# Two transformer blocks on one core: a token-major first norm, gates that read stored tiles in halves, and a delayed start of the head groups

## The chip, the cores and the metric

One Trainium2 chip; the program runs on one of its cores. The metric is the device time of one execution in microseconds (us), median of several. The engines are PE (TensorE, the matmuls), DVE (VectorE), ACT (ScalarE), POOL (GpSimd) and SP (SyncE); "ACTq" and "SPq" in the rows are the instruction streams of ACT and SP where they issue a DMA. Line numbers with an L are those of the kernel before, unless a sentence says otherwise.

## The reference, cut to what matters

The input x is 1024 tokens of 1024 features. The first block is a norm, a mixer of five branches A to E with a gate for each, and a residual; the second block has an even layer (dilated attention of four heads, pooling, a memory attention) and an odd layer. What the change touches:

```
h = rms_norm(x, g_pre)                      # x * rsqrt(mean(x*x) + 1e-6) * g_pre
...
y_d = _rglru(conv(d_x), ...) * silu(d_z)    # D: a recurrence over the tokens
mem_kv = rms_norm(mem, g_mem) @ w_mem_kv
es = einsum('bshd,bmhd->bhsm', eq, mk) * XATTN_HEAD_DIM ** -0.5
y_e = einsum('bhsm,bmhd->bshd', softmax(es), mv) * silu(e_z)
gate = sigmoid(gates)                       # 5 branches x 1024
merged = sum(gate * einsum('bsnw,nwd->bsnd', ys, w_br))
x = x + rms_norm(merged @ w_out, g_post)
...
for g in range(3):                          # even layer, each head: windows 128, 512, 2048
    num[g], m[g], den[g] = dilated_window_group(rope(q[g]), rope(k[g]), v, ...)
wts = exp(m - max(m)); out = sum(wts * num) / sum(wts * den)
y_a = out * silu(z)
```

Everything is float32.

## The kernel before

**Tiling.** Most tensors lie feature-major in SBUF: a tile is 128 features by 1024 tokens, and eight tiles (KD = 8) make x, h or the sum `acc`. `wt(j)` is tile j of the workspace `wrk` (eleven tiles), `wt(j, b)` is its half b of 512 tokens. PE works on two halves: a dense product of one weight tile (8 slices of 128 rows) is 8 steps for half 0 and 8 for half 1. Each value and each weight is split in two parts, hi and lo, and each step is three matmuls of 128x512 (hi by hi, lo by hi, hi by lo, L346), so a weight tile is 48 matmuls. The dense products write PSUM banks 0 and 1; transposes, attention and norms use banks 2 to 7. SP loads one 512 KB weight tile after the other into two slots (`w_raw`), and POOL splits them (L2327, L2332) as PE takes them.

**Order.** Nothing is reordered at run time. The program is a list of sections; a section has three threads, `dense`, `aux` and `side`, each a row of stages with a planned length in microseconds. Each engine's instruction stream is made by merging the threads by their planned times (`play`); a `yield` fraction inside a stage sets its due time. A planned length is therefore no duration; it says only what stands ahead of what. Each engine takes its stream in order, so that a matmul that waits holds all matmuls behind it, dense ones of another thread too.

**Start.** ACT issues the constants (`cst`), 37 small loads (rows of biases, gains and conv weights into `wt(0)`, `a_log`, `a_dt_bias`), then eight token-major tiles of x. After a drain (L898) PE turns the rows (L910) and then the x tiles, 8 transposes each (L917), and DVE copies them to `acc` (L927). ACT stores `acc` to DRAM as `x_fm`. Then a feature-major norm of each half: ACT squares (L504), PE sums over the features by a matmul with ones (L521), ACT takes the root (L507), DVE the reciprocal of a 128x512 tile (L529), then per feature tile DVE scales (L566), ACT rounds to the hi part (L579), DVE takes the lo part (L559). The first dense product ("A beta alpha", one weight tile) follows each part; then the two memories are turned (L1171, 8 transposes for 128 memory rows, loaded by L873), and "A project" begins (12 weight tiles).

**Gates of D and E.** Silu of z was computed before and stored to a DRAM scratch `away`. `gate_stored` (L1002) loads eight pieces of 128x512 back one by one (L1015) into the two halves of `wt(10)`; piece i waits for the multiply of piece i-2. DVE multiplies (L1025) and makes `y_hi` (L1027) and `y_lo` (L1028), and counts `y_done`; PE's y products wait for it. The D gate shares its section with E's attention: its inputs come by six fetches of 512 KB (L873), its scores are L782, its softmax L810. The E gate follows in the next section, where DVE also works out rotary angles.

**The post norm's x.** One load of `x_fm` brings x back to `wt(0..7)`, feature-major, ahead of the residual's add.

**Heads.** Four sections, one per head h: `dense` has the head's z product (one tile, Silu on ACT, L1984, into `y_spare`) and the next head's q, k and v (seven tiles); `side` has the rope on DVE (L1809 to L1813); `aux` has three attention groups and then `dilated_join` (L1888). A group turns v on PE (L1845), copies it (L1849), and runs eight attention steps (scores L782, Exp with row sum on ACT L810, transposes L795, value products L1873). The join spreads maxima over partitions (PE L1899, 24 matmuls), copies them (ACT), takes the joint maximum (DVE L1926 to L1929), the weights (ACT Exp), spreads the denominators (PE L1899, 24 more), and joins on DVE (L1941 to L1962). The next head's first L1845 waits for the join's end.

```
i = min((d, j) for j, d in enumerate(due) if d is not None)[1]   # L2287, in words: the thread with the lowest planned time goes next
```

## Time and profile before

| | us |
|---|---|
| median of 3 runs | 4007.83 |
| lowest, highest | 4007.68, 4010.31 |
| profiled execution, its own time | 4009.19 |
| span of that execution | 4007.4 |
| PE busy | 3528.8 (88%) |
| DVE / POOL / ACT busy | 1816.5 / 1577.4 / 919.5 |
| mean granted PE clock | 0.946 |

The profiled execution is 1.8 us longer than its span and 1.4 us above the median. "Idle before" in a row is the time in which the engine had nothing between its last instruction and this one; the name behind the arrow is what ended the wait. Busy time of a pipelined matmul overlaps the next, so a run of dense matmuls is read from the distance of their starts.

### The profile page before, as it was taken

Reading aid. Unit: us, or ns where it says so; the run is one execution under the profiler, and the core shown is the slowest. Engines: PE = TensorE matmul, PEld = TensorE weight load, DVE = VectorE, ACT = ScalarE, POOL = GpSimd, SP = SyncE. Lnnn points to the kernel's source line nnn. Section 1 sums busy time; section 2 is a strip of 40 time slices with the busy share of each in tenths; the row PEclk is TensorE's granted clock in tenths of the full one; section 3 lists DMA queues with packets and bytes.
Section 4 is the critical chain, followed back from the end, with each engine's and each line's share of the span. In section 5 each row is a group of like instructions: output and inputs, shape, how many; then the busy total and the mean of one; then the engine's idle time right before and its main releaser. Section 6 shows DMA issues by size and latency. Waiting matters only on the chain.

```text
span 4007.4 us, 44134 instructions
## 1 busy us (share of the span) xinstructions
PE 3528.8 (88%) x16700; PEld 2816.8 (70%) x16700; DVE 1816.5 (45%) x2349; ACT 919.5 (23%) x1687; POOL 1577.4 (39%) x2013
## 2 busy tenths in 40 slices
PE   5898999998998899979799699669677988989988
PEld 3677898886875667757577377557566766778867
DVE  3666232226795454653521646474625344122343
ACT  2324111213012342323101322223221122120021
POOL 1453453223594224533354154243323433324423
PEclk9999989999999999989899899889888999999999
DMA  3121222112121102121121110000001111111211
GB/s 133 43 66 51 64 64 64 53 56 74 46 81 49 56 24 69 37 79 40 54 76 58 55 43 27 22 27 27 22 21 64 55 29 40 47 54 37 76 40 63
DMA packets 301494, 209.03 MB, mean 52 GB/s; under 512 B 25813, under 2 KB 277593, under 8 KB 301177
## 3 DMA queue, kind: packets, MB, share of 16 engines
q1 hardware_dynamic: 270192, 131.62, 11.8%
q10 hardware_dynamic: 31113, 74.78, 5.0%
q8 instruction: 133, 2.18, 0.2%
q14 instruction: 56, 0.46, 0.0%
HBM read 172.54 MB, written 33.83 MB: 51 GB/s over the span
## 4 chain that ended last, share of the span: by engine, by line
PE 69%; DVE 16%; ACT 5%; POOL 2%; issue 2%; ACTq 2%; DMA 1%; PEld 1%; DVEq 1%; PEldq 0%; POOLq 0%
PE ps L346 51%; PE ps L1247 4%; PE ps L782 3%; DVE wrk L648 3%; DVE wrk L627 2%; POOL w_lo L2332 2%; ACT wrk L810 2%; PE ps L795 1%; PE ps L521 1%; PE ps L1599 1%; POOL w_hi L2327 1%; PE ps L1873 1%; ACTq L873 1%; DVE h_lo L559 1%; DMA wrk<-away 1%
## 5 line engine op out<-in xcount | busy, mean ns | idle before, releaser
L2327 POOL TENSOR_TENSOR w_hi<-w_raw,pool_one 128x256 fp32r<-128x256 f32 x1004 | 693.9, 720 | 2377.2 <-PE ps L346 2369.5
L346 PE MATMUL ps<-h_hi,w_hi 128*128 128x512 f32 x2928 | 1210.0, 413 | 92.5 <-POOL w_lo L2332 22.4
L346 PE MATMUL ps<-h_hi,w_lo 128*128 128x512 f32 x2928 | 1156.3, 395 | 0.0
L346 PE MATMUL ps<-h_lo,w_hi 128*128 128x512 f32 x2928 | 1156.2, 395 | 0.0
L2332 POOL TENSOR_TENSOR w_lo<-w_raw,w_hi 128x256 fp32r<-128x256 f32 x1004 | 884.2, 909 | 23.1
L346 PEld LDWEIGHTS ps<-h_hi,w_hi 128*128 128x128 f32 x2928 | 559.5, 191 | 280.8 <-issue 99.5
L346 PEld LDWEIGHTS ps<-h_hi,w_lo 128*128 128x128 f32 x2928 | 558.2, 191 | 121.5
L346 PEld LDWEIGHTS ps<-h_lo,w_hi 128*128 128x128 f32 x2928 | 560.9, 192 | 111.7 <-issue 8.9
L346 PE MATMUL ps<-y_hi,w_hi 128*128 128x512 f32 (+1 forms) x896 | 345.3, 385 | 26.9 <-issue 26.2
L346 PE MATMUL ps<-y_hi,w_lo 128*128 128x512 f32 (+1 forms) x896 | 331.2, 370 | 0.0
L346 PE MATMUL ps<-y_lo,w_hi 128*128 128x512 f32 (+1 forms) x896 | 330.9, 369 | 0.0
L346 PEld LDWEIGHTS ps<-y_hi,w_hi 128*128 128x128 f32 x896 | 172.0, 192 | 70.2 <-issue 44.2
L648 DVE SCALAR_TENSOR_TENSOR wrk<-wrk,cols 128x1023 f32<-128x1023 f32 (+29 forms) x144 | 211.3, 1533 | 0.9 <-DVE acc L458 0.2
L346 PEld LDWEIGHTS ps<-y_lo,w_hi 128*128 128x128 f32 x896 | 172.3, 192 | 30.0 <-issue 4.1
L346 PEld LDWEIGHTS ps<-y_hi,w_lo 128*128 128x128 f32 x896 | 172.0, 192 | 28.7
L1247 PE MATMUL ps<-wrk 128*128 128x128 f32 x1216 | 164.1, 285 | 1.6 <-ACT wrk L1309 0.7
L1247 PEld LDWEIGHTS ps<-wrk 128*128 128x128 f32 x1216 | 153.0, 198 | 13.2 <-DVE wrk L1347 7.5
L782 PE MATMUL ps<-wrk 128*128 128x256 f32 (+3 forms) x480 | 111.0, 381 | 56.7 <-DVEq L2278 26.4
L480 DVE TENSOR_TENSOR acc<-acc,ps 128x512 f32<-128x512 f32 x96 | 66.0, 688 | 206.4 <-PE ps L346 205.6
L462 DVE TENSOR_TENSOR wrk<-ps,wrk 128x512 f32<-128x512 f32 x64 | 44.1, 689 | 224.9 <-PE ps L346 224.4
L782 PEld LDWEIGHTS ps<-wrk 128*128 128x128 f32 (+1 forms) x480 | 88.2, 217 | 81.0 <-ACTq L2278 28.2
L446 ACT ACTIVATE wrk<-ps,cols 128x512 f32<-128x512 f32 x80 | 55.0, 689 | 376.2 <-PE ps L346 331.3
(322 smaller groups left out, 3785.3 us busy)
## 6 DMA issues: line engine op xcount, KB each, us to landing
w_raw<-in_w_in SPq DMA_DIRECT2D x87, 512.0 KB
w_raw<-in_even_w_in SPq DMA_DIRECT2D x48, 512.0 KB
away<-wrk ACTq DMA_DIRECT2D x80, 256.0 KB, 2.0
wrk<-away ACTq DMA_DIRECT2D x32, 512.0 KB
w_raw<-in_odd_w_in SPq DMA_DIRECT2D x32, 512.0 KB
x_fm<-acc ACTq DMA_DIRECT2D x2, 4096.0 KB, 12.3
w_raw<-in_w_br SPq DMA_DIRECT2D x32, 256.0 KB
w_raw<-in_even_w_out SPq DMA_DIRECT2D x24, 256.0 KB
```

The source lines that it names most:

```text
L346: mm = nc.tensor.matmul(ps[:, b, 0:n], l, r, start=(k == 0 and q == 0), stop=(k == nk - 1 and q == 2))
L446: nc.scalar.activation(wt(gt, b), ps[:, b, :], ACT.Sigmoid, bias=gate_bias(i)).then_inc(dense_free[b], 1)
L462: nc.vector.tensor_tensor(wt(gt, b), ps[:, b, :], wt(gt, b), ALU.mult).then_inc(dense_free[b], 1)
L480: nc.vector.tensor_tensor(a, a, ps[:, b, :], ALU.add).then_inc(dense_free[b], 1)
L521: nc.tensor.matmul(ps[:, bank + b, 0:n], ones, wt(sq, i % 2)[:, 0:n], start=(k == 0), stop=(k == nk - 1)).then_inc(summed.sem, 1)
L627: ch.link(nc.vector.reciprocal(wt(rs, i % 2), wt(rs, i % 2)))
L648: ins = nc.vector.scalar_tensor_tensor(dsts[i][:, s:T], tiles[i][:, 0:T - s], w, dsts[i][:, s:T], ALU.mult, ALU.add)
L782: mm = nc.tensor.matmul(S[:, u, c], l, r, start=True, stop=True)
L810: ins = nc.scalar.activation(SB[:, u, lo:256], src, ACT.Exp, bias=nmx[:, u:u + 1], scale=1.0 if has_bias else scale, accum_out=den[:, u:u ...
L1247: mm = nc.tensor.matmul(four(dst)[:, h, :], lhsT(h), rhs(h), start=True, stop=True)
L2327: ins = nc.gpsimd.tensor_tensor(hi, raw, one[:, 0:2], ALU.mult)
L2332: ins = nc.gpsimd.tensor_tensor(lo, raw, hi.bitcast(F32), ALU.subtract)
```

## The change

**Start.** The transposes now come after the scaling. ACT's queue loads the first 256 columns of the constants (the identity), the x tiles and one broadcast row of gains. The 36 small loads and the rest of the constants go to SP's queue, behind the first weight tile. Per token tile n (128 tokens by 1024 features): ACT squares with a row sum and takes a root over two tiles' sums (128x2); DVE takes that reciprocal and scales the tile by it and by the gains in one operation; PE makes 8 transposes; ACT rounds from PSUM to `h_hi`, DVE subtracts to `h_lo`. Three pairs of PSUM banks take turns. "A beta alpha" now waits for `x_parted` of the 4th tile (half 0) and the 8th (half 1). PE turns the small rows between tiles 3 and 4 in the same banks. The copy to `acc` and the first store of `x_fm` are gone.

**D and E gates.** z comes in two transfers of four pieces (1 MB each). D's: the first is issued behind the last "D root", the second in the stage behind the last scan. E's first is issued behind the fetches of E's inputs, its second at the end of E's attention. The fetches of E's inputs now wait for the whole D gate (`y_done` 7), and stand 12 us later in the plan; the positions' load and the angles wait for the whole E gate.

**Post norm's x.** x is loaded again token-major (8 loads of 512 KB), PE makes 64 more transposes and DVE 16 copies of 128x512 into the space of `y_hi` and `y_lo`.

**Heads.** A stage of 11 planned us with no work stands ahead of the groups.

The diff, cut to its core:

```diff
@@ def project
-        stage(name, dense_us(r, n), ("pe",), pe=f_pe, act=f_act)
+        stage(name, pace * dense_us(r, n), ("pe",), pe=f_pe, act=f_act)
@@ inputs
-    def load_inputs(act): ...
-    stage("load", act=load_inputs)
-    stage("turn x", 5.0, ("pe", "dve"), pe=turn_inputs, dve=copy_inputs)
-    stage("store x", act=store_x)
-    x_parted = norm_acc("norm x", "g_pre")
+    def inputs_act(act):
+        ...
+            return nc.scalar.activation(acc[:, n % 4, :], wt(1 + n), ACT.Square, accum_out=x_squares[:, n:n + 1])
+        ...
+            nc.scalar.activation(h_hi[:, :, n * P:(n + 1) * P], x_in_turn(n), ACT.Copy).then_inc(x_rounded.sem, 1)
+        act.dma_start(cst[:, 0:2 * P], A["consts"][:, 0:2 * P]).then_inc(ident_loaded, 16)
+        for n in range(NX):
+            act.dma_start(wt(1 + n), x_tiles[n]).then_inc(x_loaded[n], 16)
+            if n == 1:
+                act.dma_start(gains, A["g_pre"][0].partition_broadcast(P)).then_inc(gain_loaded, 16)
+        ...
+    def inputs_pe(pe):
+        pe.wait_ge(ident_loaded, 16)
+        for n in range(NX):
+            yield (0.2, 0.25, 0.3, 0.35, 0.5, 0.56, 0.62, 0.68)[n]
+            if n == 4:
+                pe.wait_ge(rows_in, 16 * len(small_loads))
+                ...
+                pe.wait_ge(cols_there.sem, cols_there.nth(0))
+            pe.wait_ge(x_scaled.sem, x_scaled.nth(n))
+            if n >= 3:
+                pe.wait_ge(x_parted.sem, x_parted.nth(n - 3))
+            ...
+    on("aux")
+    stage("inputs turned and normed", 40.0, pe=inputs_pe, act=inputs_act, dve=inputs_dve)
@@ dense thread, first section
+    stage("first half normed", 18.0)
+    project("A beta alpha", r_ba, ..., pace=2.4,
+            ready=lambda pe, k, b: pe.wait_ge(x_parted.sem, x_parted.nth(4 * b + 3)))
@@ gate_stored
-                    act.dma_start(wt(10, i % 2), away[place + j, :, b * HALF:(b + 1) * HALF]).then_inc(gate_loaded[i % 2], 16)
+    def load_gate(act, place, b, first):
+        ...
+        act.dma_start(gate_tiles(first), src).then_inc(gate_loaded[b], 16)
@@ D
+            if i == 3:
+                load_gate(act, at_dz, 0, 8)
+    stage("D z, second half", 0.5, act=d_gate_load)
-    fetch("E q", [...], 22.0)
+    stage("D gate read", 12.0)
+    fetch("E q", [...], 12.0, lambda act: act.wait_ge(d_done.sem, d_done.nth(7)))
+    stage("E z, first half", 0.5, act=e_gate_load)
+    stage("E z, second half", 0.5, act=e_gate_load_2)
@@ E section, aux
+        act.wait_ge(e_done.sem, e_done.nth(7))
         load(act, wt(4).bitcast(I32)[0:32, :], A["positions_2"][0].partition_broadcast(32))
+    stage("E gate read", 17.0)
@@ x back
-        load(act, wrk[:, 0:8, :], x_fm.rearrange("k p t -> p k t"))
+        for n in range(NX):
+            act.dma_start(wt(n), x_tiles[n]).then_inc(x_again, 16)
+    stage("x turned back", 45.0, pe=x_back_pe, dve=x_back_dve)
@@ heads
+        stage("head z before the groups", 11.0)
         for g in range(3):
             dilated_group(h, g)
@@ SP
+            if r.t0 == 1:
+                small_inputs()
```

How the instructions move, in three places. First, PE at the very start, after the change: L969 are the 8 transposes of a token tile, L348 the dense matmuls, L961 the turn of the small rows. In the kernel before all 64 transposes stand ahead of the 32 sums and the dense ones.

```order
L969 MATMUL ps<-cst,wrk 128x128 [waits x_parted,x_scaled]
L969 MATMUL ps<-cst,wrk 128x128 x7
L348 MATMUL ps<-h_hi,w_hi 128x512 [waits x_parted,dense_free0,tiles_split]
L348 MATMUL ps<-h_lo,w_hi 128x512
L348 MATMUL ps<-h_hi,w_lo 128x512
L348 MATMUL ps<-h_hi,w_hi 128x512 [waits x_parted]
L348 MATMUL ps<-h_lo,w_hi 128x512
L348 MATMUL ps<-h_hi,w_lo 128x512
L961 MATMUL ps<-cst,wrk 128x128 [waits x_parted,rows_in]
```

Six dense matmuls of half 0, and the wait for the small loads, now stand between the token tiles 3 and 4.

Second, ACT around the D gate; L1579 is the last root of D, L1015 a load of z, L873 the fetches for E, L446 the sigmoid of a branch gate. Before:

```order
L1579 ACTIVATE wrk<-wrk 128x1024 [waits aux_pe_stage_done]
L1015 DMA wrk<-away 128x512 [waits away_done0,away_done1,dense_dve_stage_done,dense_pe_stage_done]
L873 DMA wrk<-away 128x1024 [waits away_done0,away_done1,aux_dve_stage_done,aux_pe_stage_done]
L873 DMA wrk<-away 128x1024 x5
L1015 DMA wrk<-away 128x512
L1015 DMA wrk<-away 128x512 [waits y_done] x6
L446 ACT_TABLE_LOAD [waits loaded,dense_dve_stage_done,dense_pe_stage_done]
```

And after:

```order
L1640 ACTIVATE wrk<-wrk 128x1024 [waits aux_pe_stage_done]
L1071 DMA wrk<-away 128x4x512 [waits away_done1,away_done0]
L1071 DMA wrk<-away 128x4x512 [waits aux_dve_stage_done,aux_pe_stage_done]
L875 DMA wrk<-away 128x1024 [waits away_done1,away_done0,y_done,aux_dve_stage_done,aux_pe_stage_done]
L875 DMA wrk<-away 128x1024 x5
L448 ACT_TABLE_LOAD [waits dense_out,dense_dve_stage_done]
L448 ACTIVATE wrk<-ps,cols 128x512 [waits dense_pe_stage_done]
```

The loads of z lie ahead of the gate, and the fetches for E have moved behind all of it.

Third, PE at the second spread of a head's join (head 0). Before:

```order
L1899 MATMUL ps<-cst,small 128x128 [waits aux_dve_stage_done,aux_act_stage_done]
L1899 MATMUL ps<-cst,small 128x128 x7
L346 MATMUL ps<-h_hi,w_hi 128x512
L346 MATMUL ps<-h_lo,w_hi 128x512
L346 MATMUL ps<-h_hi,w_lo 128x512
L346 MATMUL ps<-h_hi,w_hi 128x512
L346 MATMUL ps<-h_lo,w_hi 128x512
L346 MATMUL ps<-h_hi,w_lo 128x512
L1899 MATMUL ps<-cst,small 128x128 x8
```

And after, where the same spread is L2011:

```order
L2011 MATMUL ps<-cst,small 128x128 [waits aux_dve_stage_done,aux_act_stage_done]
L2011 MATMUL ps<-cst,small 128x128 x23
L348 MATMUL ps<-h_hi,w_hi 128x512 [waits dense_free0,tiles_split]
L348 MATMUL ps<-h_lo,w_hi 128x512
L348 MATMUL ps<-h_hi,w_lo 128x512
```

Behind the last spread now stands the next head's whole z product (48 matmuls, ahead of its groups) and 6 matmuls of the tile after it; before, 18 dense matmuls and 6 of z stood there. Between the two spreads 36 dense matmuls stand where 48 stood, and none inside the second. The first L1845 of the head follows (L1957 after the change).

## Rows read from the trace of the kernel before

**Rows 1.** The page: busy time of the engines

```profile
PE 3528.8 (88%) x16700; PEld 2816.8 (70%) x16700; DVE 1816.5 (45%) x2349; ACT 919.5 (23%) x1687; POOL 1577.4 (39%) x2013
```

**Rows 2.** Windows at the start (last columns: PE clock, DMA share, GB/s)

```profile
10.00:14.00 4.00, 0.00 (x0) 0.00 (x0) 0.00 (x0) 0.00 (x0) 3.92 (x7) 1.00 0.06 15
...
22.00:30.00 8.00, 7.52 (x41) 6.82 (x41) 5.05 (x5) 0.00 (x0) 0.00 (x0) 1.00 1.04 400
```

**Rows 3.** Timeline (start, length, work), PE: memory's turn, A project's first matmul

```profile
84.08 1.97 PE L1171 MATMUL ps<-cst,wrk 128*128 128x128 f32 x8 [5.18 <-ACTq L2278]
86.13 0.79 PE L346 MATMUL ps<-h_hi,w_hi 128*128 128x512 f32 x1
```

**Rows 4.** Groups, 3900 us to the end: the final norm, token-major

```profile
L2244 DVE SCALAR_TENSOR_TENSOR wrk<-ps,small,wrk 128x1024 f32<-128x1024 f32 x8 | 10.3, 1284 | 0.3
```

**Rows 5.** Groups, 0 to 86 us: count, busy us, mean ns, idle before

```profile
L559 DVE TENSOR_TENSOR h_lo<-wrk,h_hi 128x512 fp32r<-128x512 f32 x16 | 10.9, 691 | 3.7 <-ACT h_hi L579 3.7
```

**Rows 6.** Timeline, PE: transposes of two x tiles

```profile
31.80 2.19 PE L917 MATMUL ps<-cst,wrk 128*128 128x128 f32 x16 [0.28 <-DVE acc L927]
```

**Rows 7.** Timeline, PE: dense matmuls at the start

```profile
60.37 0.63 PE L346 MATMUL ps<-h_hi,w_lo 128*128 128x512 f32 x1
60.80 0.63 PE L346 MATMUL ps<-h_hi,w_hi 128*128 128x512 f32 x1
```

**Rows 8.** Timeline, all engines: the second memory's load and turn

```profile
153.69 0.82 ACTq L873 DMA_DIRECT2D wrk<-in_mem  x2
...
160.21 1.97 PE L1171 MATMUL ps<-cst,wrk 128*128 128x128 f32 x8 [10.44 <-ACTq L2278]
```

**Rows 9.** Timeline, DVE: two pieces of the D gate

```profile
1753.54 0.69 DVE L1025 TENSOR_TENSOR wrk<-wrk 128x512 f32<-128x512 f32 x1 [9.83 <-DMA wrk<-away]
...
1755.34 0.68 DVE L1025 TENSOR_TENSOR wrk<-wrk 128x512 f32<-128x512 f32 x1
```

**Rows 10.** Timeline, ACT's queue in the D gate

```profile
1741.13 2.83 ACTq L873 DMA_DIRECT2D wrk<-away  x6
1743.98 20.86 ACTq L1015 DMA_DIRECT2D wrk<-away  x7
```

**Rows 11.** Timeline, PE: the first score matmuls of E

```profile
1769.86 1.62 PE L782 MATMUL ps<-wrk 128*128 128x256 f32 x3 [26.41 <-DVEq L2278]
```

**Rows 12.** Timeline, ACT's queue in the E gate

```profile
1937.96 27.28 ACTq L1015 DMA_DIRECT2D wrk<-away  x7
```

**Rows 13.** Timeline, PE: the first y product of E

```profile
1970.40 0.77 PE L346 MATMUL ps<-y_hi,w_hi 128*128 128x512 f32 x1 [23.30 <-issue]
```

**Rows 14.** Windows: x's return; head 0; head 1's groups, its join

```profile
2118.00:2202.00 84.00, 83.65 (x364) 68.71 (x363) 0.37 (x1) 9.08 (x16) 36.02 (x56) 0.99 0.15 44
2362.00:2532.00 170.00, 134.30 (x704) 112.85 (x704) 96.22 (x108) 43.83 (x84) 63.47 (x65) 0.91 0.10 28
2540.00:2600.00 60.00, 56.70 (x294) 48.40 (x293) 22.70 (x39) 20.21 (x44) 17.32 (x24) 0.97 0.09 27
2660.00:2702.00 42.00, 14.39 (x84) 12.04 (x84) 39.21 (x27) 5.09 (x5) 16.26 (x13) 0.74 0.09 26
```

**Rows 15.** Waits of PE, 2300 to 3100 us: total, times, longest

```profile
PE ps L1845 <- DVEq L2278: 83.2, 3, 28.1
...
PE ps L782 <- ACT wrk L810: 19.2, 12, 4.0
PE ps L1899 <- DVEq L2278: 15.1, 5, 11.0
```

**Rows 16.** Timeline, PE: 14 matmuls of head 0's first spread

```profile
2475.79 1.73 PE L1899 MATMUL ps<-cst,small 128*128 128x128 f32 x14
```

**Rows 17.** Timeline, DVE, head 0's join: rope (L1809) between two multiplies

```profile
2498.25 1.23 DVE L1941 TENSOR_TENSOR acc<-ps,acc 128x1024 f32<-128x1024 f32 x1 [0.81 <-PEq L2278]
...
2503.89 1.28 DVE L1809 STREAM_SHUFFLE y_spare<-wrk 32x1024 f32<-32x1024 f32 x1
...
2511.31 1.93 DVE L1941 TENSOR_TENSOR wrk<-ps,acc 128x1024 f32<-128x1024 f32 x1 [0.24 <-DVE wrk L1812]
```

More of the change, by code:

```diff
@@ L371, in out_taken, with project @@
         eng.wait_ge(dense_free[b], t + 2)
-    def project(name, r, dst, bias=None, rhs=None, n=HALF, before=None, ready=None):
+    def project(name, r, dst, bias=None, rhs=None, n=HALF, before=None, ready=None, pace=1.0):
         def f_pe(pe):
@@ new lines, in _hybrid, with x_in_turn, squares, squares_of_two @@
+    x_parted = sig.take("x_parted", NX)
+    x_squares = small[:, 0:8]
+    gains = acc[:, 7, :]
+    def x_in_turn(n):
+        b = 2 + 2 * (n % 3)
+        return ps[:, b:b + 2, :].rearrange("p a (d t) -> p (a d) t", t=P)
+    def inputs_act(act):
+        ch = chains["act"]
+        def squares(n):
+            act.wait_ge(x_loaded[n], 16)
+            return nc.scalar.activation(acc[:, n % 4, :], wt(1 + n), ACT.Square, accum_out=x_squares[:, n:n + 1])
+        def squares_of_two(g):
+            squares(2 * g)
+            ch.link(squares(2 * g + 1))
+            s = x_squares[:, 2 * g:2 * g + 2]
+            nc.scalar.activation(s, s, ACT.Sqrt, bias=EPS, scale=1.0 / D).then_inc(x_rooted.sem, 1)
+        def rounded(n):
+            act.wait_ge(x_turned.sem, x_turned.nth(n))
+            nc.scalar.activation(h_hi[:, :, n * P:(n + 1) * P], x_in_turn(n), ACT.Copy).then_inc(x_rounded.sem, 1)
+        act.dma_start(cst[:, 0:2 * P], A["consts"][:, 0:2 * P]).then_inc(ident_loaded, 16)
+        for n in range(NX):
+            act.dma_start(wt(1 + n), x_tiles[n]).then_inc(x_loaded[n], 16)
+            if n == 1:
+                act.dma_start(gains, A["g_pre"][0].partition_broadcast(P)).then_inc(gain_loaded, 16)
+        act.wait_ge(table_ready.sem, table_ready.nth(0))
+        nc.scalar.activation(warm, warm, ACT.Sqrt)
+        squares_of_two(0)
+        squares_of_two(1)
+        rounded(0)
+        yield 0.4
+        rounded(1)
+        squares_of_two(2)
+        rounded(2)
+        rounded(3)
+        yield 0.6
+        squares_of_two(3)
+        for n in range(4, NX):
+            rounded(n)
+        act.wait_ge(rows_in, 16 * len(small_loads))
+        act.wait_ge(consts_in, 16)
@@ L1126, in ba_turn @@
         mm.then_inc(logits_turned.sem, 1)
-    stage("A turn", 24.0, pe=ba_turn)
+    stage("A turn", 10.0, pe=ba_turn)
     def ba_copy(dve):
@@ L1157, in _hybrid @@
     on("side")
+    stage("inputs normed", 36.0)
     for which, (mem, g_mem) in enumerate(((A["mem"], "g_mem"), (A["mem_2"], "g_mem_2"))):
         def m_load(act, mem=mem):
[L1160 removed]
+            act.wait_ge(x_parted.sem, x_parted.nth(NX - 1))
             for j in range(2):
```

188 lines of the change are left out of this document (115 added, 73 removed).

## The prediction, on record before the changed kernel ran

> **What bounds the kernel now.** I read the page first: PE is busy 88% of the span, DVE 45%, ACT 23%, POOL 39% [rows 1]. PE takes its stream in order, so a change is worth what it takes out of PE's idle time or adds to PE's work; a faster DVE or DMA elsewhere is worth nothing. Then I looked at PE's timeline for its waits, and at what ended each. Four of the places that the change touches carry real idle time. At the start, the first matmul of A project begins at 86.13, behind a last wait of 5.18 for a memory tile [rows 3]; all before it is a serial preparation with one weight tile of dense work in it. In the D gate PE waits 26.41 us and goes on at 1769.86 [rows 11]. In the E gate it waits 23.30 us, until 1970.40 [rows 13]. At the joins of heads 0 to 2 it waits 83.2 us in three waits [rows 15]. The fifth place is the opposite: while x comes back for the post norm, PE is busy 83.65 of 84 us [rows 14], so work added there is paid.
>
> **Units.** Warm dense matmuls: 364 in 83.65 us [rows 14], 0.23 us each, 11.0 us for a weight tile. Cold ones start 0.43 apart [rows 7]. The profiled execution took 4009.2 us, span 4007.4, median 4007.8; I take the sum from the profiled one and subtract 1.4 for the median.
>
> **Start.** Removed: the feature-major norm with its sums over features, the copy to `acc`, the store, and the small loads from ACT's queue. While ACT issued these, the DMAs ran at 15 GB/s, against 400 when x flowed [rows 2]: the issue was the limit, not the transfer. In the new chain ACT issues 10 transfers, estimated done by 7.5 us; a root's table, two squares of 128x1024 and a root follow, so DVE begins to scale at about 11.6. Then DVE sets the pace: a scaling of 128x1024 is 1.28 [rows 4], a subtraction twice 0.69 [rows 5], 2.65 a tile, 21.2 for eight. Three gaps come on top: behind tiles 3 and 7 the subtraction waits for PE's 8 transposes (1.1, since 16 took 2.19 [rows 6]) and ACT's rounding of 128x1024 (about 1.0), 2.1 each; between them stand six cold dense matmuls (2.6), the turn of the small rows and the copy of columns, about 4. So tile 7 is parted at 11.6 + 21.2 + 4.2 + 4 = 41. Behind it are 24 matmuls of "A beta alpha", half of them cold: 12 x 0.43 + 12 x 0.23 = 7.9. A project starts at about 49, against 86.13: 37. The first memory's turn, 1.97 [rows 3], now stands later and without its wait, which takes back 2: **-35**. From below: with x landing smoothly and warm matmuls at once, -40. From above: with four more us until the first tile is there, -31. The first weight tile is needed at 26 and the second at 49; some 6.3 MB in all at 400 GB/s are 16 us, so I take both as there, though SP's 37 small issues stand between them.
>
> The Trainium skill, page "DMA: Bandwidth & Descriptors", section "Issuing engines are not separate DMA queues", says that transfers of different issuers run on the same 16 DMA engines and interleave, and that spreading them saves only issue time. By it the small loads on SP slow x down rather than pass beside it; that is the rival of the late x below.
>
> **The memories.** The second memory's load is issued at 153.69 and its turn waits 10.44, until 160.21 [rows 8]. The load's place moves earlier against PE's turn; I estimate half of the wait gone, -5 (0 to -8), and about 3 lost where the first chunk of A, whose inputs come from DVE, now has fewer dense matmuls ahead (0 to 5). Together **-2**.
>
> **D gate.** A piece costs DVE 1.80 (distance of the two rows [rows 9]), eight are 14.4. Today the queue on ACT stretches this over 20.86 us of waits [rows 10]. After the change both halves are loaded ahead; DVE runs 1741.2 to 1755.7. The fetches for E, issued at 1741.13 today, now wait for that end. They take 2.83 to issue [rows 10], and 3.1 MB at 400 GB/s [rows 2] are 8 us with about 2 until the first lands: E's inputs are there at 1766. PE's scores then start 3.9 earlier than 1769.86, with 54 instead of 30 dense matmuls done before them (24 x 0.23 = 5.5): **-9.3**, between -6 and -12. Queued behind the new wait on ACT are the sigmoids of the D merge; PE fills two PSUM banks and would stand until 1756, so they are late for 12 us, but PE's y products need `y_done` until then too.
>
> **E gate.** The loads took 27.28 us from 1937.96 [rows 12]. z is now there; eight pieces from 1937.3 end at 1951.7, and the first y product follows 1.1 later, at 1952.8 instead of 1970.40: **-17.6**. Bounds: -20 with y products that start at a piece's end in half 0, -15 if a rotary stage still gets between. ACT's wait for the whole gate ahead of the positions holds the sigmoids until 1951.7, no longer than PE's own wait.
>
> **x comes back.** 64 transposes on a PE with no idle: 4 x 2.19 = **+8.8** [rows 6]; up to 10.6 cold, 8.0 at best. The 16 copies of 128x512 (0.69 each, like the subtraction [rows 5]) are hidden by a DVE that is busy 0.37 of these 84 us [rows 14]; without that cover they would add 11. The transfer is as large as before.
>
> **Heads.** The stage of 11 shifts the groups against the dense work. In head 0's join a rope of the next head stands between two multiplies: it begins at 2503.89, and the next multiply starts at 2511.31 [rows 17], 7.4 us on the path. It moves ahead of the second spread, into DVE's wait for PE and ACT. The 12 dense matmuls inside the second spread leave it (12 x 0.23 = 2.7; 14 spread matmuls alone take 1.73 [rows 16]). A join is 10.1 shorter, and PE's idle time of 27.7 in it falls by this and by the 30 dense matmuls that go behind the spread. That dense work leaves the groups, which are bound by PE: 56.70 busy of 60 us in head 1's [rows 14]. Three head cycles (one is the 170 us window of head 0 [rows 14]) lose 10.1 each: -30.3. Head 3's groups carry 186 dense matmuls instead of 234: -11. Head 0 starts later: 54 matmuls (12.4) stand where a wait of 7.2 was and 1.4 of them before, +3.6. Fewer matmuls as cover expose more of the softmax waits, today 19.2 in 12 waits [rows 15]; I take +3. Sum **-35**. The nearest rows bound it: between -17 (only the 30 matmuls' shift counts, join unchanged) and -42 (no new exposure, table loads of Silu out of the softmax).
>
> **Sum.** -35 - 2 - 9.3 - 17.6 + 8.8 - 35 = -90.1. Profiled 4009.2 - 90.1 = 3919.1, median 3917.7, rounded to **3918**.
>
> **The rivals.**
> *The groups give it back.* Without their filler, PE waits for ACT and DVE in each attention step, and what the join gains is spent. For: softmax waits exist at all (19.2, and 15.1 for spreads [rows 15]). Against: 0.97 clock and 3.3 us of idle in 60 [rows 14]. Heads -17 instead of -35: 3936.
> *Late x.* The gains row, the constants, two weight tiles and 37 small loads share the DMAs with x: 6.3 MB at 400 GB/s are 16 us, and if all x tiles land together at 16 to 18 instead of in order, the first scaling starts at 18 to 20, and the memory's turn does not recover it: +8 to +11, 3927.
> *The E fetches land late.* They stood ahead of the gate and now stand behind it. At half the rate they take 16 us and 2 more, and with their issue and the first step of the attention the scores come at 1775; the D gate gains nothing: 3927.
> *Slower.* The granted clock. In the 42 us of a join it is 0.74, in the groups 0.97 [rows 14]. If the shorter cover opens gaps in every step so that the groups too run at 0.74, 56.7 busy us become 74.3, +17.6 in 60, and +34 in the 116 us of groups of a head. Four heads cost 136: 4054. It decides from 22.5 us a head on, a mean clock in the groups below about 0.81. Against it: 36 to 48 matmuls fewer of some 330, and the waits seen are at most 4.0 [rows 15].
> The Trainium skill, page "TensorE: Matmul & The Clock Gate", section "HAM oscillation — how this bites in real kernels", warns that waits between bursts drop the clock to 1.2 GHz again and again. The join's 0.74 agrees in kind; the groups' 0.97 says that today's short waits don't do it.
> *Nothing.* The long waits have another end behind them (a sigmoid, a DMA) and the total stays within 8 us.
>
> **Chances.** Forecast 0.62; groups give back 0.17; late x 0.11; late fetches 0.05; slower 0.03; nothing 0.02. A difference of 0.2%, 8 us, is about what a measurement tells from none. The first four are faster by more: faster 0.95, same 0.02, slower 0.03. Range: all lower bounds together (-40, -8, -12, -20, +8, -42) give -114, 3894; all upper ones (-31, +5, -6, -15, +10.6, -17) give -53, 3954. All at once is unlikely on the upper side: 3892 to 3950.
>
> **What would show it.** Right: A project's first matmul at 47 to 52; E's first scores near 1766 minus about 37, with PE's wait before them under 15; the E gate's wait near 5; x's return 9 us longer with DVE copies inside; waits of PE at the first v turn of heads 1 to 3 near 12 instead of 27.7, and cycles near 160. Wrong: squares that start after 14 us; tiles parted later than 3 us apart; L1957 waits as long as before with the groups shorter, or groups with a clock under 0.9; a new wait at the z products for a weight tile or for a Silu, since a Silu behind the softmax on ACT would hold PSUM.

## The result, and where the time went

| | predicted | measured |
|---|---|---|
| median of the changed kernel, us | 3918 (3892 to 3950) | 3955.79 (3947.18 to 3961.24, 4 runs) |
| beside the kernel before, us | -90 | 4007.76 before, ratio 0.9868, interval 0.9854 to 0.9883: -53 (-47 to -59) |
| profiled execution | 3919.1 | 3957.16, span 3955.3 |

The direction was right and the size was not: 53 us instead of 90. The time lies 6 us above the range, and 2 above the sum of all its upper bounds (3954). Of the executions told below one, of the last kernel, took 11834 us at a granted clock of 0.32; the ratios leave it out. The page of the changed kernel, to be read beside [rows 1]:

```profile
span 3955.3 us, 44173 instructions
...
PE 3541.3 (90%) x16732; PEld 2842.2 (72%) x16732; DVE 1811.4 (46%) x2344; ACT 897.8 (23%) x1667; POOL 1580.2 (40%) x2013
```

PE's busy time grew by 12.5 us, 6.7 of it in the part where x returns (the windows below), and the span fell by 52.1. To see where, I took events of PE's stream that both traces have and subtracted their times. Each number below is how much earlier, or later, the changed kernel got through that part of the program.

| part, ended by | before, at | after, at | gain in this part | forecast |
|---|---|---|---|---|
| start to branch D, to PE's last wait for a weight tile ahead of the D gate | 1736.36 | 1701.60 | -34.8 | -37 |
| D gate and E's attention, to the begin of PE's wait in the E gate | 1947.10 | 1905.56 | -6.8 | -9.3 |
| E gate and its merge, to the first matmul behind the merge | 2103.16 | 2056.68 | -4.9 | -17.6 |
| x's return, to the post norm's first sum | 2203.45 | 2163.71 | +6.7 | +8.8 |
| post norm | 2276.23 | 2235.70 | -0.8 | 0 |
| heads, to the end of the wait behind head 3's join | 3036.08 | 2982.74 | -12.8 | -35 |
| rest | 4007.4 | 3955.3 | +1.2 | 0 |

Before rounding the rows sum to -52.1. Two of the terms carry the error, 12.7 us at the E gate and 22.2 in the heads. One trace of each kernel stands behind the table: in a second trace of the changed one, told below, the lead differs by up to 8 us inside the first row and by 1.3 at the end.

**The start** came out nearly as forecast. The DMA windows answer to [rows 2]: while ACT issued small loads the DMAs had stood at 15 GB/s, and now the same stretch moves x.

```profile
2.00:8.00 6.00, 0.00 (x0) 0.00 (x0) 0.00 (x0) 1.85 (x3) 1.62 (x3) 1.00 1.04 351
10.00:14.00 4.00, 1.90 (x9) 1.89 (x10) 3.54 (x3) 2.50 (x5) 2.54 (x3) 1.00 1.04 403
```

DVE begins to scale at 10.25 (forecast 11.6), copies the columns at 28.34, and has parted the last tile at 42.43 (forecast 41). A project starts at 48.64 (forecast 49, [rows 3] before), and the memory's turn has no wait.

```profile
10.25 3.37 DVE L987 SCALAR_TENSOR_TENSOR wrk<-wrk,small,acc 128x1024 f32<-128x1024 f32 x2
...
28.34 0.56 DVE L995 COPY cols<-ps 128x388 f32<-128x388 f32 x1 [3.92 <-PE ps L961]
...
41.20 1.23 DVE L980 TENSOR_TENSOR h_lo<-ps,h_hi 128x1024 fp32r<-128x1024 f32 x1 [1.11 <-ACT h_hi L922]
```

```profile
48.64 0.47 PE L348 MATMUL ps<-h_hi,w_hi 128*128 128x512 f32 x1 [0.37 <-issue]
...
50.11 1.04 PE L1232 MATMUL ps<-cst,wrk 128*128 128x128 f32 x8
```

**The D gate.** The rows of ACT answer to [rows 10], those of PE to [rows 11]; L1085, L1087 and L1088 are the gate's three operations, L875 the fetches for E, L448 the merge's sigmoid.

```profile
1724.63 2.81 ACTq L875 DMA_DIRECT2D wrk<-away  x6
1727.55 1.28 ACT L448 ACT_TABLE_LOAD   x1 [29.05 <-issue]
1728.85 0.69 ACT L448 ACTIVATE wrk<-ps,cols 128x512 f32<-128x512 f32 x1
```

```profile
1729.63 0.76 PE L348 MATMUL ps<-y_hi,w_hi 128*128 128x512 f32 x1 [16.84 <-issue]
...
1736.69 3.75 PE L784 MATMUL ps<-wrk 128*128 128x256 f32 x8 [4.16 <-DVEq L2391]
```

PE waits 16.84 and then 4.16 instead of 26.41. The product of y's half 0 needs only the first four pieces, each of its steps one of them; DVE has done the four at 1714.9. It starts at 1729.63, 0.1 us behind the end of the sigmoid, since ACT takes the first gate tile out of PSUM only behind the whole gate. And the pieces are slower than [rows 9] told, 1.8 us each at first and up to 3.1 later, 18 for the eight. The second piece, and the fifth:

```profile
1708.88 0.69 DVE L1085 TENSOR_TENSOR wrk<-wrk 128x512 f32<-128x512 f32 x1
1709.60 0.43 DVE L1087 CAST y_hi<-wrk 128x512 fp32r<-128x512 f32 x1
1710.06 0.69 DVE L1088 TENSOR_TENSOR y_lo<-wrk,y_hi 128x512 fp32r<-128x512 f32 x1
...
1714.84 1.10 DVE L1085 TENSOR_TENSOR wrk<-wrk 128x512 f32<-128x512 f32 x1
1715.97 0.72 DVE L1087 CAST y_hi<-wrk 128x512 fp32r<-128x512 f32 x1
1716.73 1.09 DVE L1088 TENSOR_TENSOR y_lo<-wrk,y_hi 128x512 fp32r<-128x512 f32 x1
```

**The E gate.** ACT's rows answer to [rows 12], PE's to [rows 13]:

```profile
1914.60 0.34 ACTq L875 DMA_DIRECT2D wrk<-in_positions  x1
1914.99 0.69 ACT L448 ACTIVATE wrk<-ps,cols 128x512 f32<-128x512 f32 x1 [27.68 <-DVEq L2391]
1918.22 0.69 ACT L448 ACTIVATE wrk<-ps,cols 128x512 f32<-128x512 f32 x1 [2.54 <-DMA wrk<-in_positions]
```

```profile
1915.78 0.77 PE L348 MATMUL ps<-y_hi,w_hi 128*128 128x512 f32 x1 [10.22 <-issue]
...
1928.32 0.64 PE L348 MATMUL ps<-h_hi,w_hi 128*128 128x512 f32 x1 [4.10 <-DVE wrk L464]
```

The wait fell from 23.30 to 10.22, but not to 5. It ends not with a piece but behind a sigmoid, which had waited 27.68. Then the second sigmoid waits for the positions' transfer, the rotary angles (L1733 to L1748) hold DVE until 1927.5, and PE waits 4.10 for a multiply of the merge. Of the gain at the gate, 13.1, the merge gives back 8.1: 2 more in this wait (4.1 where 2.1 was), 2 in waits for weight tiles (4.6 where 2.8 was), and the rest, some 4 us, goes with more time at the half clock (the lower of the two granted levels, 1.2 instead of 2.4 GHz, 0.50 in the windows).

**x's return and a head.** The windows are of the kernel before and of the changed one, the same part of the program, and then head 1 of the changed one, to be read beside head 0's in [rows 14]:

```profile
2103.10:2203.40 100.30, 94.91 (x384) 74.48 (x384) 15.03 (x14) 10.31 (x18) 43.28 (x64) 0.91 0.20 62
```

```profile
2056.60:2163.70 107.10, 101.60 (x448) 80.56 (x449) 25.34 (x30) 10.34 (x18) 43.32 (x64) 0.93 0.19 59
2488.30:2654.20 165.90, 137.92 (x704) 116.37 (x704) 95.33 (x107) 41.51 (x82) 63.21 (x64) 0.92 0.09 26
```

64 matmuls more, 6.8 us more; DVE's 10 us of copies are beside PE's work. Head 1 is a cycle of 165.9 where it was 170.3, with the same 704 matmuls, and PE is busy 2.9 us longer in it.

### The profile page after: what moved, and what is told of

Its sections match the earlier page's. It is cut to its first block, busy times and chain, and to the rows that moved or that the text cites. A ratio compares the mean times of both kernels' runs of the same rounds, so it can differ in the third digit from the quotient of the medians.

```text
span 3955.3 us, 44173 instructions
## 1 busy us (share of the span) xinstructions
PE 3541.3 (90%) x16732; PEld 2842.2 (72%) x16732; DVE 1811.4 (46%) x2344; ACT 897.8 (23%) x1667; POOL 1580.2 (40%) x2013
## 4 chain that ended last, share of the span: by engine, by line
PE 71%; DVE 15%; ACT 5%; issue 3%; POOL 3%; ACTq 1%; DMA 1%; PEld 1%; DVEq 0%; PEldq 0%; POOLq 0%
PE ps L348 53%; PE ps L1308 5%; PE ps L784 3%; DVE wrk L650 3%; DVE wrk L629 2%; ACT wrk L812 2%; POOL w_lo L2453 2%; PE ps L797 1%; PE ps L1666 1%; PE ps L523 1%; POOL w_hi L2448 1%; PE ps L1985 1%; DVE wrk L837 1%; DVE small L840 1%; PE ps L676 1%
## 5 line engine op out<-in xcount | busy, mean ns | idle before, releaser
L348 PE MATMUL ps<-h_hi,w_hi 128*128 128x512 f32 x2928 | 1210.0, 413 | 97.2 <-POOL w_lo L2453 23.7
L348 PE MATMUL ps<-h_lo,w_hi 128*128 128x512 f32 x2928 | 1157.8, 395 | 0.0
L348 PE MATMUL ps<-h_hi,w_lo 128*128 128x512 f32 x2928 | 1157.7, 395 | 0.0
L2453 POOL TENSOR_TENSOR w_lo<-w_raw,w_hi 128x256 fp32r<-128x256 f32 x1004 | 893.4, 918 | 23.2
L348 PEld LDWEIGHTS ps<-h_hi,w_hi 128*128 128x128 f32 x2928 | 560.4, 191 | 280.6 <-issue 105.7
L348 PEld LDWEIGHTS ps<-h_hi,w_lo 128*128 128x128 f32 x2928 | 559.5, 191 | 122.1
L348 PEld LDWEIGHTS ps<-h_lo,w_hi 128*128 128x128 f32 x2928 | 561.5, 192 | 112.8 <-issue 8.9
L348 PE MATMUL ps<-y_hi,w_hi 128*128 128x512 f32 (+1 forms) x896 | 349.6, 390 | 30.5 <-issue 29.7
L348 PE MATMUL ps<-y_hi,w_lo 128*128 128x512 f32 (+1 forms) x896 | 335.1, 374 | 0.0
L348 PE MATMUL ps<-y_lo,w_hi 128*128 128x512 f32 (+1 forms) x896 | 334.9, 374 | 0.0
L348 PEld LDWEIGHTS ps<-y_hi,w_hi 128*128 128x128 f32 x896 | 175.7, 196 | 74.9 <-issue 48.7
L348 PEld LDWEIGHTS ps<-y_lo,w_hi 128*128 128x128 f32 x896 | 176.0, 196 | 30.0 <-issue 3.8
L348 PEld LDWEIGHTS ps<-y_hi,w_lo 128*128 128x128 f32 x896 | 175.6, 196 | 29.0
L1308 PEld LDWEIGHTS ps<-wrk 128*128 128x128 f32 x1216 | 157.0, 202 | 13.7 <-DVE wrk L1408 6.7
L448 ACT ACTIVATE wrk<-ps,cols 128x512 f32<-128x512 f32 x80 | 55.2, 689 | 383.3 <-PE ps L348 340.4
L426 DVE TENSOR_TENSOR wrk<-wrk 128x512 f32<-128x512 f32 x56 | 45.1, 805 | 196.2 <-ACT wrk L415 196.0
```

Source lines behind the costliest of these rows:

```text
L348: mm = nc.tensor.matmul(ps[:, b, 0:n], l, r, start=(k == 0 and q == 0), stop=(k == nk - 1 and q == 2))
L426: ch.link(nc.vector.tensor_tensor(o(j, b), o(j, b), wt(sz, b), ALU.mult))
L448: nc.scalar.activation(wt(gt, b), ps[:, b, :], ACT.Sigmoid, bias=gate_bias(i)).then_inc(dense_free[b], 1)
L1308: mm = nc.tensor.matmul(four(dst)[:, h, :], lhsT(h), rhs(h), start=True, stop=True)
L2453: ins = nc.gpsimd.tensor_tensor(lo, raw, hi.bitcast(F32), ALU.subtract)
```

## Experiments: each part alone

The three parts of the change touch different code, so each can be put into the kernel before by itself. First the heads.

```diff
+        stage("head z before the groups", 11.0)
         for g in range(3):
             dilated_group(h, g)
```

> The kernel before with one edit: the stage of 11 planned us ahead of each head's groups. Theory of the forecast (the groups are bound by PE, so dense matmuls that leave them shorten them): 35 us faster, head 3's groups 11 us shorter than before. Theory from the two traces (the groups are bound by the chain of waits between PE, ACT and DVE, in which dense matmuls stood for nothing): 12 to 14 us faster, head 3's groups as long as before (105 us), groups of heads 0 to 2 at 108 to 110 instead of 107, joins 6 to 9 shorter.

Measured: 3998.91, ratio 0.9978 (0.9967 to 0.9988), 9 us faster. In its trace the heads' part alone gives 11.4 (748.4 us where 759.9 were). Head 3's groups take 104.9 us, as before (104.5). The forecast's 35 is out.

The gates' part alone (everything of the diff on `gate_stored`, `load_gate`, the fetches of E and the positions):

> The kernel before with the gates' part alone (z of D and E in two transfers, the fetches and the rotary angles behind the gates). Theory of the forecast: 27 us faster (9.3 at D, 17.6 at E). Theory from the traces (E's gate gains 13, but the merge behind it gives 8 back, as the positions' transfer and the angles now stand between the sigmoids and the multiplies): 12 us faster, with a wait of about 4 for a multiply of the merge.

Measured: 3992.01, ratio 0.9967 (0.9956 to 0.9979), 13 us faster, as the traces had told; the forecast's 27 is out.

The start's part alone (the token-major norm, the small loads on SP, x's second load and its transposes):

> The kernel before with the token-major first norm, and the token-major reload of x that it needs. Forecast: 35 + 2 - 8.8 = 28 us faster. The trace of the changed kernel shows 34.8 - 6.8 = 28, but with more of the chunk phase at the half clock than before. If that excess belongs to the change, 28 again; if it differs from run to run, between 28 and 40.

Measured: 3979.07, ratio 0.9928 (0.9911 to 0.9944), 29 us faster. The three by themselves sum to 51, the whole change to 53: within the intervals, which are 4 to 7 us to each side, they neither help nor hinder one another, and the miss lies inside two of them.

The changed kernel a second time:

> The changed kernel once more, to see which parts of its trace repeat. If the half clock from 389 to 406 us and its like in the chunk phase follow from the order of work, the second trace has them at the same places, and about 78 us of half clock between the first chunk and the last. If they are chance, their sum moves by 20 us or more and the time by up to half of that.

Measured: 3955.28, ratio 0.9871 (0.9855 to 0.9888). The heads repeat to 0.1 us in nearly every group. In the chunk phase (branch A goes over the tokens chunk by chunk, from 305 to 879 us) the half clock comes mostly at the same places of the program, but for other lengths: together 78 us in the first trace, 55 in the second, 79 in that of the start alone, against 51 in the kernel before. The sum moved by more than 20, so by the expectation it is largely chance. The other traces say the same: in this phase those of the later experiments, which leave the phase alone, have 55 to 85 us, and the two that keep the old start, only_gates and only_heads, 44 and 65. At half speed an excess of 4 to 27 us costs 2 to 14 of the start's gain, as an estimate; the forecast's "-2" for the chunks did not have that. The second trace led the first by 8 us at the end of the chunks, 5 at the D gate and 1.3 at the end.

## Experiments: what ended the waits at the two gates

The first attempt moved ACT's instructions only. In `e_later` the positions' load (with its wait for the whole gate) is planned later, in `d_later` the fetches of E.

```diff
-    stage("E gate read", 17.0)
+    stage("E gate read", 34.0)
```

> The changed kernel with the stage that holds back the positions' load 34 instead of 17 planned us long: on ACT the first two sigmoids of the E merge now stand ahead of the wait for the whole E gate. Theory: it was ACT's wait that held PE (both PSUM banks full until ACT takes them), so the y product of half 0 starts when its own four pieces are done, about 10 us earlier, and the wait of 4 for the multiply goes: PE's waits at the two places fall from 14.3 to under 4, the time by 8 to 15. Rival (DVE's pieces set the y product's start): under 3 us.

Measured: 3951.89, ratio 0.9864 (0.9845 to 0.9882), 4 us below the changed kernel in the median, which the intervals don't tell from nothing. ACT and PE in the E gate:

```profile
1918.31 0.69 ACT L448 ACTIVATE wrk<-ps,cols 128x512 f32<-128x512 f32 x1 [27.30 <-DVEq L2391]
1918.44 0.34 ACTq L875 DMA_DIRECT2D wrk<-in_positions  x1
```

```profile
1919.09 0.77 PE L348 MATMUL ps<-y_hi,w_hi 128*128 128x512 f32 x1 [9.85 <-issue]
```

The sigmoid now stands ahead of the positions' load, and still starts at 1918.31 behind a wait of 27.30; PE still waits 9.85. The theory was half wrong: ACT did hold PE, but the load's wait did not hold ACT.

```diff
-    stage("D gate read", 12.0)
+    stage("D gate read", 22.0)
```

> The changed kernel with the stage ahead of E's fetches 22 instead of 12 planned us long: the first sigmoid of the D merge stands ahead of ACT's wait for the whole D gate, and E's scores stand 66 dense matmuls later on PE. Theory: PE's wait of 16.8 falls to 2 to 4, and the scores' wait grows little since the dense matmuls cover the fetch: 8 to 12 us faster. Rival: the attention of E, 66 dense matmuls later against its chain, ends later and its end holds the E gate: nothing gained.

Measured: 3954.04, ratio 0.9873 (0.9856 to 0.9889), no difference to the changed kernel. PE at the first y product of D, whose wait fell from 16.84 and not to the 2 to 4 of the theory:

```profile
1721.17 0.77 PE L348 MATMUL ps<-y_hi,w_hi 128*128 128x512 f32 x1 [14.14 <-issue]
```

What held the sigmoid stands in `stage` and `thread_part`: an engine that enters a stage waits until the other engines have ended all earlier stages of the thread, except the engines that name themselves in `ahead`. `merge` names PE alone. So ACT's first sigmoid waited for DVE's gate stage, all eight pieces, whatever stood around it. The kernel `y_early` lifts this, keeps e_later's 34 planned us ahead of the positions, and has 26 ahead of the fetches where d_later had 22 (the fetches' own stage is 2 instead of 12):

```diff
+                    elif prev:
+                        act.wait_ge(prev.sem, prev.nth(14 + b))
...
-        stage(name, pace * dense_us(r), ("pe",), pe=f_pe, act=f_act, dve=f_dve)
+        stage(name, pace * dense_us(r), ("pe", "act") if prev else ("pe",), pe=f_pe, act=f_act, dve=f_dve)
```

> The changed kernel with ACT's stage of the D and the E merge no longer waiting for DVE's stage before it (the whole gate), only for its tile's last reader in the merge before; both first sigmoids stand ahead of the wait for the gate, E's fetches and the positions behind them. The kernel e_later moved the sigmoid in the order alone, and PE still waited 9.9. Theory: what held PE's y product was the stage wait on ACT, which asks for all eight pieces where the product of half 0 needs four. PE's waits at the two y products fall from 16.8 and 10.2 to under 4 and under 3, and 12 to 20 us are gained. Rival (transfers or DVE set the end of both places): under 4 us.

Measured: 3939.32, ratio 0.9827 (0.981 to 0.9844), 16 us below the changed kernel. PE at the first step of D's y product and at two steps of its half 1, then at E's scores, and at the last step of E's y product:

```profile
1716.36 0.39 PE L348 MATMUL ps<-y_hi,w_hi 128*128 128x512 f32 x1
...
1721.70 0.47 PE L348 MATMUL ps<-y_hi,w_hi 128*128 128x512 f32 x1 [2.03 <-DVE y_lo L1091]
...
1724.73 0.79 PE L348 MATMUL ps<-y_hi,w_hi 128*128 128x512 f32 x1 [2.10 <-DVE y_lo L1091]
```

```profile
1740.58 2.04 PE L787 MATMUL ps<-wrk 128*128 128x256 f32 x4 [8.84 <-DVEq L2395]
```

```profile
1911.29 0.53 PE L348 MATMUL ps<-y_hi,w_hi 128*128 128x512 f32 x1 [1.95 <-DVE y_lo L1091]
```

The products of half 0 start without a wait, D's at 1716.36, and what waits are left, about 2 us each, are steps of half 1 that wait for their own piece (`y_lo`, L1091). The scores wait 8.84 instead of 4.16, since their inputs come no earlier; the sum at D is 13.0 instead of 21.0, at E 2 instead of 10.2. At E only the stage wait separates this kernel from e_later, and it decides: that settles the cause there. At D the fetches stand 4 planned us later than in d_later as well.

## Experiments: what the groups of a head are bound by

The join did what was foreseen: its part of the cycle, from the first spread to the next v turn, fell from 62.8 to between 54.3 and 56.6. The groups grew instead of shrinking. The table gives the three groups of a head, from PE's first v turn of each to the next, in us, with the dense matmuls in them.

| kernel, head | group 1 | group 2 | group 3 | sum | join |
|---|---|---|---|---|---|
| before, head 1 | 39.6 (108) | 38.2 (90) | 29.7 (90) | 107.6 | 62.8 |
| changed, head 1 | 36.4 (96) | 45.0 (96) | 27.9 (84) | 109.3 | 56.6 |
| heads_22, head 1 | 42.5 (90) | 42.8 (90) | 40.8 (90) | 126.1 | 61.6 |
| rope_later, head 1 | 36.9 (96) | 39.5 (96) | 27.9 (84) | 104.3 | 54.3 |
| before, head 3 | 39.1 (108) | 46.0 (126) | 19.4 (0) | 104.5 | |
| changed, head 3 | 41.0 (114) | 43.3 (72) | 20.6 (0) | 105.0 | |
| bare_head3, head 3 | 31.2 (0) | 31.6 (0) | 20.4 (0) | 83.2 | |

Groups 1 and 3 of head 1 did shorten, by about what their dense matmuls are. Group 2 has 6 more and is 6.8 us longer. In head 3 the 48 dense matmuls that left were worth nothing. Its windows, before and changed, say where their 11 us went:

```profile
2873.60:2978.10 104.50, 91.47 (x459) 77.38 (x459) 25.47 (x55) 30.98 (x71) 25.59 (x40) 0.91 0.09 26
```

```profile
2819.60:2924.60 105.00, 85.48 (x410) 72.56 (x410) 24.91 (x55) 25.83 (x66) 20.45 (x32) 0.83 0.07 21
```

PE is busy only 6.0 us less, and idle 6.5 more. The 5 us of busy time that did not go are matmuls that took longer, at a granted clock of 0.83 where it was 0.91. So about half of this loss is waits and half is clock.

The next kernel takes all dense work out of head 3:

```diff
         else:
-            r_px = run(2, *both(w2, C2_X))
-            project("pool x", r_px, acc_at, before=lambda act, j, b: head_free(act, 4))
...
     section()
     on("dense")
+    r_px = run(2, *both(w2, C2_X))
+    project("pool x", r_px, acc_at, before=lambda act, j, b: head_free(act, 4))
...
-    stage("pool sums", 26.0, dve=p_dve)
+    stage("pool sums", 70.0, dve=p_dve)
```

> The changed kernel with the product of pool x (4 weight tiles, 192 dense matmuls) moved out of head 3's section into the next one, and the stage of the pool sums made longer so that it waits there. It measures head 3's groups without dense matmuls. If they are bound by PE, they shorten by nearly all of the 42 us of moved work and the time stays the same. If they are bound by their chain, they stay near 100 us and the kernel gets slower by 30 or more.

Measured: 3974.31, ratio 0.9921 (0.9904 to 0.9937), 19 us slower than the changed kernel. The window of head 3's groups without dense matmuls:

```profile
2812.40:2895.50 83.10, 46.11 (x224) 41.03 (x224) 23.22 (x55) 21.23 (x58) 0.00 (x0) 0.68 0.00 0
```

Without any dense work the groups take 83 us and not 63 (105 less 42): the chain of scores, softmax, transposes and value products needs that long by itself at the clock that it was granted, 0.68. How much of the 83 belongs to that clock was not separated; if all of PE's 46 busy us stood on the chain, some 15 of them would, as an estimate (46.11 x 0.32), and 68 are still more than 63. 186 dense matmuls (42 us) in it cost 22. Neither end of the expectation holds: a dense matmul in a group of head 3 is paid by half on the average. That is why the forecast's "bound by PE" failed; it was read from a window of 60 us with 56.7 busy, in which the waits are short because the dense work fills them.

The other way, a longer shift:

```diff
-        stage("head z before the groups", 11.0)
+        stage("head z before the groups", 22.0)
```

> The changed kernel with 22 instead of 11 planned us ahead of each head's groups: some 48 more dense matmuls stand behind the last spread and as many fewer in the groups. Theory of the forecast (groups bound by PE): the join's rest of 14 us is filled, 10 to 11 us a head gained, about 30 in all. Theory from the traces (groups bound by their chain): the join's wait falls to about 3, the groups stay at 108 to 110 or grow only by lost matmuls covered by waits, and of the dense work that is moved into the join what the groups lose is not returned: 0 to 15 us gained, with longer waits for softmax and rope.

Measured: 4032.19, ratio 1.006 (1.0039 to 1.008): 76 us slower than the changed kernel, and 24 slower than the one before. Both theories missed this. The dense matmuls in the groups are nearly as many (270 instead of 276), and yet each head's groups take 15 to 17 us more and the join 5 to 7 more (no dense work is left between its two spreads, where PE now waits 13.4). In head 1's groups PE is busy 104.4 us where it was 98.5, at a granted clock of 0.89 where it was 0.95, and idle 21.8 where it was 10.8: two thirds of the 16.8 us are waits, one third goes with the clock. DVE in head 0's third group shows what waits:

```profile
2427.69 0.01 DVE L1921 LOAD_MASK_SELECT y_spare<-wrk  x1 [4.10 <-ACT wrk L1899]
...
2433.83 0.88 DVE L837 SCALAR_TENSOR_TENSOR wrk<-ps,cst 128x128 f32<-128x128 f32 x4
```

L1921 is the rope of the next head. It waits 4.10 for a dense tile that ACT must bring (L1899), runs 6.1 us, and only behind it comes the bias add of the softmax (L837). The same pattern is in the changed kernel's second group; first DVE there, then the same place of the kernel before:

```profile
2547.91 0.01 DVE L1921 LOAD_MASK_SELECT y_spare<-acc  x1 [8.36 <-ACT acc L1899]
...
2552.36 1.64 DVE L1924 TENSOR_TENSOR acc<-acc,y_spare 32x1024 f32<-32x1024 f32 x1
2554.04 1.42 DVE L837 SCALAR_TENSOR_TENSOR wrk<-ps,cst 128x256 f32<-128x256 f32 x4
```

```profile
2585.64 1.34 DVE L1809 STREAM_SHUFFLE y_spare<-acc 32x1024 f32<-32x1024 f32 x1
...
2592.67 1.42 DVE L835 SCALAR_TENSOR_TENSOR wrk<-ps,cst 128x256 f32<-128x256 f32 x4 [0.54 <-PE ps L795]
```

Before, the rope began at 2585.64, with its tile there and PE still at the scores, and the bias add then waited 0.54. After the change DVE waits 8.36, ropes until 2554.04, and the softmax begins behind it. PE's waits of that step, and the join's:

```profile
2488.32 1.94 PE L1957 MATMUL ps<-cst,wrk 128*128 128x128 f32 x8 [14.28 <-issue]
```

```profile
2539.40 4.13 PE L784 MATMUL ps<-wrk 128*128 128x128 f32 x16 [2.64 <-ACT wrk L812]
...
2559.49 0.74 PE L797 MATMUL ps<-cst,wrk 128*128 128x128 f32 x4 [3.63 <-DVE small L856]
```

The stage of 11 planned us moved the attention against dense work and ropes; the rope's tile is now finished on PE behind the scores that stand ahead of it. The mend is to move the ropes too:

```diff
-            rope(h + 1, r_qk, 20.8, HEAD_PACE)
+            rope(h + 1, r_qk, 24.8, HEAD_PACE)
```

> The changed kernel with the ropes' stage starting 4 planned us later (24.8 instead of 20.8), so that on DVE the second rope of each next head stands behind the softmax's operations of its step and no longer ahead of them. Theory: in the second group of heads 0 to 2 DVE waits 8.4 us for a dense tile, then ropes for 6.1 us while the scores lie ready, and the group takes 45.0 instead of 38.2; with the rope behind, the group falls to 38 to 41, 4 to 6 us a head, 12 to 18 in all. Rival (the groups are long because dense matmuls have left them and the clock falls): the group stays at 45, no gain.

Measured: 3937.33, ratio 0.983 (0.9813 to 0.9846), 18 us below the changed kernel. DVE at the same step:

```profile
2536.62 1.42 DVE L837 SCALAR_TENSOR_TENSOR wrk<-ps,cst 128x256 f32<-128x256 f32 x4 [6.35 <-PE ps L797]
...
2542.49 0.77 DVE L856 COPY small<-small 128x4 f32<-128x4 f32 x1 [1.15 <-ACT wrk L812]
2543.18 0.01 DVE L1921 LOAD_MASK_SELECT y_spare<-acc  x1
```

The bias add waits for PE's transposes and not for a rope, and the rope comes behind the softmax. Group 2 is 39.5 instead of 45.0 with the same 96 dense matmuls, so the rival (missing filler, falling clock) is out for these 5.5 us; the group's time at the half clock fell with it, from 6.8 us to 3.4. The cycles of heads 0 to 2 are 158.0, 158.6 and 159.9 us, which is the forecast's "near 160". Head 3 has no next head whose rope could stand in the way; its groups stay at 104.7, so the 11 us that were forecast there are lost to something else, the waits and the clock of its windows above.

Both mends together:

> The changed kernel with both mends: ACT's merge stages of D and E free of the wait for the whole gate (and the fetches and positions behind the first sigmoids), and the ropes 4 planned us later. If the two losses are separate, as their places in the program say, their gains add: 16 + 18 = 34 us below the changed kernel, 3921. If they share something (the clock, the lead of the dense work), less than 28.

Measured: 3921.76 in the median, ratio 0.9775 (0.9762 to 0.9787). The gains add, 16 + 18 = 34. This kernel beats both, and lies 4 us above what was forecast for the change itself.

## The prediction, step by step

**Start, -37 with the memories: right, by -34.8, and partly by luck.** A project's start, 48.64 for 49, is a sum whose errors cancel: the first scaling came 1.4 us early, the chain to the last parted tile took 32.2 us and not 29.4, and the matmuls behind it 6.2 and not 7.9. The gaps at the tiles 3 and 7 were 1.1 each instead of 2.1, and the subtraction took 1.22 and not 1.38, but four more waits for the rounding, 0.50 to 1.94, were not in the sum. Of "late x" nothing showed: the third and fourth tile waited 0.78 and 0.24 us. The split into -35 and -2 was not right in its parts: at the first chunk of A the changed kernel led by 46.7, and it gave back 14 until the end of the chunks, much of it at the half clock, of which the second trace shows less.

**D gate, -9.3: nearly right, by -6.8.** The scores came at 1736.69, 33.2 earlier instead of 37 + 3.9; a piece cost up to 3.1 instead of 1.80, so the gate took 18.0 us instead of 14.4. But the sentence "PE's y products need `y_done` until then too" was wrong: those of half 0 need only the first four pieces. In y_early they start at 1716.36, without a wait, where the gate ends at 1728.3.

**E gate, -17.6: the mechanism failed, -4.9.** The step was "ACT's wait ... holds the sigmoids until 1951.7, no longer than PE's own wait". PE's own wait would have been for the first four pieces, not for eight: DVE had done them at 1904.2, before PE arrived at 1905.56, and PE then stood 10.2 us for the sigmoid. The pieces took 18.0 us in place of 14.4, and the positions and the angles, which had been spread inside the old wait, now stood in front of the merge: 8.1 given back. That work of DVE moved out of a wait comes back later in the same engine's stream was not in the sum at all.

**x's return, +8.8: right in kind, +6.7.** The transposes stood between dense ones and took about 0.10 each instead of 0.14 (eight from 2095.88 to the next matmul at 2096.66).

**Heads, -35: wrong, -12.8.** What was right in kind: the joins (three of them, -6.2 to -8.5 each, forecast -10.1) and head 0's later start (+4.0, forecast +3.6). What was wrong: "that dense work leaves the groups, which are bound by PE". Of the "30 dense matmuls" only 12 a head left the groups (288 before, 276 after); the others came out of the join itself. The groups of heads 0 to 2 became 1.3 to 2.2 us longer instead of shorter, and head 3's -11 was 0.5 the other way. In parts: 7.6 us are missing in the joins, 5.2 in the groups of heads 0 to 2 and 11.5 in head 3; against these the sum had allowed 3 for exposed waits. The rival "the groups give it back" named the outcome, with -17 in place of -12.8. In heads 0 to 2 the mechanism was another, DVE's order of ropes and softmax, 5.5 us a head; in head 3 the rival's mechanism is seen, 6.5 us more of idle time, beside 5 us that go with the clock, and no run separates the two. The "-17" as the upper bound of the range was therefore too good, and with E's term 12.7 short the time left the range.

**The slower rival**, groups at a clock under 0.9, was not what happened in heads 0 to 2 (0.95 in head 1's), but it was in head 3, 0.83. heads_22 went that way everywhere: 27 us at the half clock in a head's groups instead of 10. That the waits came first and the clock followed is the likely reading, since twice as much of the loss is waits as busy time, but it was not tested.

## What to carry to other kernels

Where the order is merged from planned times, moving one thread moves it against both others: list for every in-order engine what now stands ahead of the critical chain and whether its input is there, not only on the engine that waits. A wait that a stage inherits from its thread can be longer than the work it protects; ask which pieces the consumer needs. And a window in which PE is 95% busy does not say that work taken out of it is gained; the test is the same window without that work, and its clock has to be read beside its length.
